# Key norm and group norm of the recurrent rounds in token form, spread back by products

## The reference, cut to what matters

```python
kk = heads(k * k_k)
kk = kk / jnp.maximum(jnp.sqrt(jnp.sum(kk * kk, axis=-1, keepdims=True)), 1e-12)
...
wkv = wkv7_scan(rh, heads(decay), kh, vh, -kk, kk * ah)
mean = jnp.mean(wkv, axis=-1, keepdims=True)
var = jnp.mean(jnp.square(wkv - mean), axis=-1, keepdims=True)
y = ((wkv - mean) * lax.rsqrt(var + GN_EPS)).reshape(B, S, RWKV_WIDTH) * ln_w + ln_b
bonus = jnp.sum(rh * kh * r_k, axis=-1, keepdims=True) * vh
return (y + bonus.reshape(B, S, RWKV_WIDTH)) * g
```

## Time and profile before

| what | value |
|---|---|
| median of 3 runs | 2893.79 us (2889.46 to 2896.81) |
| the profiled execution's own time | 2894.06 us |
| its span in the profile | 2892.3 us |
| TensorE (PE) busy | 2612.6 us, 90% |
| VectorE (DVE) busy | 1232.6 us, 43% |
| ScalarE (ACT) busy | 1094.6 us, 38% |
| GpSimd (POOL) busy | 811.4 us, 28% |

### The profile page before, as it was taken

How to read it: one execution, slowest core, us unless ns; L and a number is a source line. 1 busy time by engine, 2 the same in 40 slices (tenths; PEclk the granted TensorE clock), 3 DMA queues, 4 the chain that set the end, 5 groups by cost and what they waited for, 6 DMA issues and landing times. The chain is left out here.

```text
span 2892.3 us, 49485 instructions
## 1 busy us (share of the span) xinstructions
PE 2612.6 (90%) x19266; PEld 2052.9 (71%) x19266; DVE 1232.6 (43%) x1836; ACT 1094.6 (38%) x1686; POOL 811.4 (28%) x342
## 2 busy tenths in 40 slices
PE   8999979989898969669999999989978889898997
PEld 6887857868686857558878887768865567676665
DVE  3221024464646446442142221056836642674652
ACT  4433224333333323444434332243244432335441
POOL 3444423413232303004434444412210002232002
PEclk9999989999999989879999999999989999999999
DMA  4232322312121202013323223311110001122001
GB/s 135 88 100 90 101 71 86 90 51 86 55 90 51 88 25 80 8 47 102 102 73 95 94 94 102 101 37 51 58 44 1 1 8 51 45 73 65 1 1 65
DMA packets 51998, 188.39 MB, mean 65 GB/s; under 512 B 5760, under 2 KB 6016, under 8 KB 51712
## 3 DMA queue, kind: packets, MB, share of 16 engines
q1 hardware_dynamic: 50688, 181.74, 19.9%
q10 hardware_dynamic: 1152, 4.26, 0.4%
HBM read 183.88 MB, written 2.10 MB: 64 GB/s over the span
## 5 line engine op out<-in xcount | busy, mean ns | idle before, releaser
L2324 POOL TENSOR_TENSOR WLO<-RAW,WHI 128x1024 fp32r<-128x1024 f32 x334 | 806.3, 2414 | 2041.9 <-ACT WHI L297 2041.9
L297 ACT ACTIVATE WHI<-RAW 128x1024 fp32r<-128x1024 f32 x336 | 355.8, 1059 | 973.7 <-PE psum L311 774.4
L309 PE MATMUL psum<-HHI,WHI 128*128 128x512 f32 x1000 | 403.2, 403 | 41.7 <-DVE HLO L395 15.0
L310 PE MATMUL psum<-HLO,WHI 128*128 128x512 f32 x1000 | 396.5, 397 | 0.0
L311 PE MATMUL psum<-HHI,WLO 128*128 128x512 f32 x1000 | 396.4, 396 | 0.0
L309 PEld LDWEIGHTS psum<-HHI,WHI 128*128 128x128 f32 x1000 | 189.6, 190 | 91.6 <-issue 45.9
L309 PE MATMUL psum<-H2HI,WHI 128*128 128x512 f32 (+1 forms) x536 | 197.7, 369 | 31.2 <-DVE H2LO L393 21.6
L310 PEld LDWEIGHTS psum<-HLO,WHI 128*128 128x128 f32 x1000 | 189.4, 189 | 47.0 <-issue 3.2
L311 PEld LDWEIGHTS psum<-HHI,WLO 128*128 128x128 f32 x1000 | 189.2, 189 | 45.0
L310 PE MATMUL psum<-H2LO,WHI 128*128 128x512 f32 (+1 forms) x536 | 192.0, 358 | 0.0
L311 PE MATMUL psum<-H2HI,WLO 128*128 128x512 f32 (+1 forms) x536 | 191.7, 358 | 0.0
(11 more groups left out here) (381 smaller groups left out, 4995.9 us busy)
## 6 DMA issues: line engine op xcount, KB each, us to landing
RAW<-in_wstream SPq DMA_DIRECT2D x336, 512.0 KB, 3.5
X<-in_xT SPq DMA_DIRECT2D x8, 256.0 KB, 6.7
out_T<-OUT SPq DMA_DIRECT2D x4, 512.0 KB, 2.6
W3S<-in_lora ACTq DMA_DIRECT2D x5, 384.0 KB, 3.1
XC<-in_ctxT ACTq DMA_DIRECT2D x1, 1024.0 KB, 4.8
TRIG<-in_trig ACTq DMA_DIRECT2D x1, 960.0 KB, 6.8
FCC<-in_first SPq DMA_DIRECT2D x1, 576.0 KB, 8.6
LVL<-in_levels SPq DMA_DIRECT2D x1, 384.0 KB, 9.0
```

The lines of the kernel that those rows point to most:

```text
L297: act.activation(WHI[:, q % 2, :], RAW[:, q % 2, :], ACT.Copy).then_inc(rounded, 1)
L309: pe.matmul(out, tile_of(WHI, slot, u), hi(kt), start=first and last[0], stop=False)
L310: pe.matmul(out, tile_of(WHI, slot, u), lo(kt), start=False, stop=False)
L2324: pool.tensor_tensor(WLO[:, s, :], RAW[:, s, :], WHI[:, s, :].bitcast(F32), ALU.subtract)\
```

## The change

The two norms keep one number per token and head instead of a copy on each of 64 partitions. `token_sums` makes the tile of squares the stationary operand, 128 tokens at a time, and multiplies by two columns of the head mask: four products of 128 stationary columns and 2 moving ones, whose result is 128x8 (tokens on partitions; four blocks, two heads). Square root, maximum and reciprocal run on 128x8 in a new tile ROOT. `spread` brings the result back to 128x512 in PSUM by eight products, each with one column of ROOT repeated 64 times as stationary operand and the 128x128 identity as moving one. "kk" and "n0" then read their factor from PSUM.

```diff
+        ROOT = ra("ROOT", [P, 2, 2 * BLOCKS])
...
                 def low_ranks(p):
-                    pe.wait_ge(*A.before(f"sd_{p}", i))
-                    pe.wait_ge(*V.before(f"dd_{p}", i))
+                    pe.wait_ge(*V.before(f"n0_{p}", i))
...
+                def token_sums(name, p, src, *waits):
+                    for w in waits:
+                        pe.wait_ge(*w)
+                    for b in range(BLOCKS):
+                        mm = pe.matmul(SETS[p].B[0][:, 2 * b:2 * b + 2], src[:, b * P:(b + 1) * P], two_heads, start=True, stop=True)
+                    mm.then_inc(*S.inc(f"{name}_{p}"))
+                def spread(name, p, *waits):
+                    for w in waits:
+                        pe.wait_ge(*w)
+                    pe.sem_inc(tensor_ready)
+                    for b in range(BLOCKS):
+                        for h in range(2):
+                            mm = pe.matmul(SETS[p].B[0][h * HD:(h + 1) * HD, b * P:(b + 1) * P],
+                                           ROOT[:, p, 2 * b + h:2 * b + h + 1].to_broadcast([P, HD]), eye, start=True, stop=True)
+                    mm.then_inc(*S.inc(f"{name}_{p}"))
...
                 for p in TWO:
-                    head_sums("kkss", p, SETS[p].B[0], SETS[p].E1[:, :], A.at(f"kksq_{p}", i))
-                whole(streamed(1), streamed(2))
+                    token_sums("kkss", p, SETS[p].E1, A.at(f"kksq_{p}", i))
+                whole(streamed(1))
+                for p in TWO:
+                    spread("kkb", p, V.at(f"kkinv_{p}", i))
+                whole(streamed(2))
...
                 for p in TWO:
-                    head_sums("var", p, SETS[p].B[0], SETS[p].DSQ[:, :], A.at(f"dsq_{p}", i))
+                    token_sums("var", p, SETS[p].DSQ, A.at(f"dsq_{p}", i))
                 whole(tail)
+                for p in TWO:
+                    spread("varb", p, V.at(f"rinv_{p}", i))
...
-                    run("e3", p, d.E3[:, :], d.SG[:, :], ACT.Exp, V.at(f"cprev_{p}", i), V.at(f"kk_{p}", i), scale=-DECAY)
+                    run("e3", p, d.E3[:, :], d.SG[:, :], ACT.Exp, V.at(f"cprev_{p}", i), scale=-DECAY)
...
-                    run("kkn", p, d.E3[:, :], d.B[0], ACT.Sqrt, S.at(f"kkss_{p}", i))
+                    run("kkn", p, ROOT[:, p, :], d.B[0][:, 0:2 * BLOCKS], ACT.Sqrt, S.at(f"kkss_{p}", i))
...
-                    run("sd", p, SETS[p].E1[:, :], SETS[p].B[0], ACT.Sqrt, S.at(f"var_{p}", i), scale=1.0 / HD, bias=EPS[:, 1:2])
+                    run("sd", p, ROOT[:, p, :], SETS[p].B[0][:, 0:2 * BLOCKS], ACT.Sqrt, S.at(f"var_{p}", i), scale=1.0 / HD, bias=EPS[:, 1:2])
...
+                def unit_root(p):
+                    ts(f"kkmax_{p}", ROOT[:, p, :], ROOT[:, p, :], 1e-12, None, ALU.max, None, A.at(f"kkn_{p}", i))
+                    inverse(f"kkinv_{p}", ROOT[:, p, :], V.at(f"kkmax_{p}", i))
                 def unit_key(p):
-                    ts(f"kkmax_{p}", d.E3[:, :], d.E3[:, :], 1e-12, None, ALU.max, None, A.at(f"kkn_{p}", i))
-                    inverse(f"kkinv_{p}", d.E3[:, :], V.at(f"kkmax_{p}", i))
-                    stt(f"kk_{p}", d.KK[:, :], d.RKV[:, 1, :], col("k_k", i * 2 + p), d.E3[:, :], ALU.mult, ALU.mult, V.at(f"kkinv_{p}", i))
+                    stt(f"kk_{p}", d.KK[:, :], d.RKV[:, 1, :], col("k_k", i * 2 + p), d.B[0], ALU.mult, ALU.mult, S.at(f"kkb_{p}", i))
...
+                unit_root(0)
+                unit_root(1)
                 unit_key(0)
...
                 for p in TWO:
+                    inverse(f"rinv_{p}", ROOT[:, p, :], A.at(f"sd_{p}", i))
+                for p in TWO:
-                    inverse(f"rinv_{p}", d.E1[:, :], A.at(f"sd_{p}", i))
-                    tt(f"n0_{p}", dv, dv, d.E1[:, :], ALU.mult, V.at(f"rinv_{p}", i))
+                    tt(f"n0_{p}", dv, dv, d.B[0], ALU.mult, S.at(f"varb_{p}", i))
```

More of the change, by code:

```diff
@@ L601, in block_kernel @@
         ROWS = ra("ROWS", [4, ROW])
+        ROOT = ra("ROOT", [P, 2, 2 * BLOCKS])
         named = lambda p, *names: [f"{n}_{p}" for n in names]
-        rw_pe = named(0, "zw", "za", "g") + named(1, "zw", "za", "g") + ["kkss_0", "kkss_1", "bonus_0"]
+        rw_pe = named(0, "zw", "za", "g") + named(1, "zw", "za", "g") + ["kkss_0", "kkss_1", "kkb_0", "kkb_1", "bonus_0"]
         rw_pe += named(0, "toka", "tokb", "tokk", "tokv", "m1", "al", "m2") + ["bonus_1", "t1_0"] + named(1, "toka", "tokb", "tokk", "tokv", "m1")
@@ L609, in block_kernel @@
         rw_pe += [f"xt{LEVELS - 1}_1", "z_0", "turn4", "y_1", "q_0", "z_1", "gt_0", "q_1", "gt_1"]
-        rw_pe += [f"s{n}_{p}" for n in range(CHUNKS - 1) for p in TWO] + ["turn5", "o_0", "o_1", "mean_0", "mean_1", "var_0", "var_1"]
+        rw_pe += [f"s{n}_{p}" for n in range(CHUNKS - 1) for p in TWO] + ["turn5", "o_0", "o_1", "mean_0", "mean_1", "var_0", "var_1", "varb_0", "varb_1"]
         rw_act = named(0, "sg", "aa", "gg") + named(1, "sg", "aa", "gg") + ["kksq_0", "kksq_1", "pb0", "kkn_0", "kkn_1", "e1_0", "e2_0", "pb1"]
@@ L619, in block_kernel @@
             rw_dve += named(p, "dr", "r", "dv", "v", "csum", "cprev")
-        rw_dve += named(0, "kkmax", "kkinv", "kk", "kp", "rk", "rt", "bb", "at", "bt", "ktl", "bon")
+        rw_dve += named(0, "kkmax", "kkinv") + named(1, "kkmax", "kkinv")
+        rw_dve += named(0, "kk", "kp", "rk", "rt", "bb", "at", "bt", "ktl", "bon")
         first_level = ("al", "xi", "xi0", "m2a", "m2b", "xit", "xit0")
-        rw_dve += named(1, "kkmax", "kkinv", "kk", "kp", "rk") + ["m1a_0", "m1b_0"] + named(1, "rt", "bb", "at")
+        rw_dve += named(1, "kk", "kp", "rk") + ["m1a_0", "m1b_0"] + named(1, "rt", "bb", "at")
         rw_dve += named(0, *first_level) + named(1, "bt", "ktl", "bon", "m1a", "m1b") + ["x1_0", "xt1_0"]
@@ L627, in block_kernel @@
         rw_dve += [f"xt{LEVELS - 1}_1", "q_0", "gt_0", "q_1", "gt_1"] + [f"s{n}_{p}" for n in range(CHUNKS - 1) for p in TWO]
-        rw_dve += ["dd_0", "dd_1", "rinv_0", "n0_0", "n1_0", "n2_0", "yf_0", "rinv_1", "n0_1", "n1_1", "n2_1", "yf_1", "mod_sum", "mods"]
+        rw_dve += ["dd_0", "dd_1", "rinv_0", "rinv_1", "n0_0", "n1_0", "n2_0", "yf_0", "n0_1", "n1_1", "n2_1", "yf_1", "mod_sum", "mods"]
         def h_hi(t):
@@ L695, in rwkv_tensor @@
             e2 = lambda s: FCC[s, FC["eye2"]:FC["eye2"] + HD]
+            two_heads = heads.rearrange("p (h n) -> p h n", n=HD)[:, :, 0]
             unit = lambda t: lambda s, n: t[s, n * CHUNK:(n + 1) * CHUNK]
@@ L765, in tokens @@
                     pe.wait_ge(*V.at(f"ktl_{p}", i))
-                    pe.wait_ge(*A.at(f"kkn_{p}", i))
                     unit_products(unit(d.B[0]), unit(d.AR[:, 0, :]), lambda s, n: e2(s), f"toka_{p}")
```

## The result

The changed kernel takes 2863.13 us (median, 2860.44 to 2864.4) against 2892.99 for the kernel before: a ratio of 0.990, 95% interval 0.9886 to 0.9914. That is 30 us less; the forecast was 2892.0 and its range ended at 2879. The execution profiled took 2860.44 us, the fastest of its four, with a span of 2858.6.

What follows compares the result with a forecast made beforehand. TensorE fills most of a round; its idle lies largely at the seams, behind a relay of engines. Round 1 -0.6, three seams -0.5 each, last end +3.9: 1.8 us gained, 2892.0; own range 2888 to 2896, whole 2879 to 2897.

Steps and rivals of the forecast that it cites:

- makes POOL ask at 634.2: Start of a round: POOL's subtraction asks while VectorE is in cprev_1 until 634.5, with kkmax next.
- the meeting: Seams of rounds 2 to 4: kkmax comes while POOL subtracts and waits 2.4 us.
- The rule itself: VectorE beside POOL: a two-port operation, like one with two SBUF inputs, is held to POOL's end; kkmax taken as such.
- it is held: Seams: kkmax waits 2.4 us for POOL and each seam loses 0.5 us; chance 0.45.
- 0.3 of distance is thin: Seams: VectorE 0.3 us away from kkmax being through before POOL asks, which would give rival 2's time.
- rival 2: Seams: kkmax isn't held and the clock stays; 3.7 us gained per seam, 2879.4 us in all; chance 0.25.
- The end: End of round 4: mods and TensorE's start come 3.9 us earlier, at half clock as before.
- Round 1: Round 1: TensorE pays 0.3 us for sums and 1.9 for spreads, gets 1.6 back at m1_0; loses 0.6.
- n0, n1, spreads and the last wait: n0 escapes POOL (about 0.69 us), n1 is held (some 2.2); spread pairs take 1.9; MOD wait 10 or less.
- behind m1_0 nothing changes: Rest of each round after m1_0: no change, so a shift there is carried through the round.
- Rival 3: low_ranks behind the var spreads and streamed(2): TensorE loses its clock, 2 us a stretch; 2904 us; chance 0.06.

Runs made afterwards that it cites:

- early: The changed kernel with the var spreads moved ahead of the tail block's last two of eight units; 2866.67 us, ratio to before 0.9919.
- pad: The kernel before with 64 empty semaphore increments in TensorE's stream behind streamed(0) of each round; 2889.65 us, ratio to before 1.0007.
- after_b: The changed kernel run once more with the same code; 2866.87 us, ratio to before 0.9908.
- key_only: The changed kernel with its group norm put back, only the key norm in token form; 2882.79 us, ratio to before 0.998.
- filler: The kernel before with the 24 products of streamed block 0 done twice; 2894.16 us, ratio to before 1.0013.
- group_only: The changed kernel with its key norm and e3's wait for kk put back; 2875.0 us, ratio to before 0.9956.
- pad16: The kernel before with 16 empty semaphore increments in TensorE's stream behind streamed(0); 2894.57 us, ratio to before 1.0013.
- held: The changed kernel with one more reciprocal, 400 elements wide, on VectorE ahead of the first kkmax; 2876.56 us, ratio to before 0.9966.

## Why the prediction was wrong

**The step that failed at the seams** is "Rounding (0.3 behind it, 1.06 long) makes POOL ask at 634.2. VectorE, 3.9 earlier, is then in "cprev_1", until 634.5." VectorE's side was exact: from the end of yf to kkmax I had 15.7 us, measured 15.65 (611.56 to 627.21). TensorE's side was not: from yf's end to POOL's second ask 15.4 forecast, 18.1 measured (611.56 to 629.64). Of the 2.7 us, 2.2 lie in low_ranks: its idle at the loop's turn was 2.71 where I took 1.5 from a round in which long products covered it, and the two pairs took 7.1 us until the block (607.73 to 614.84) where I had 6.1, with the granted clock at 0.57 in 608 to 612. So POOL asked after kkmax instead of just before it, in all three seams (by 2.4, 0.6 and 2.5 us; the 0.6 is seam 2, where low_ranks ran at full clock). A small delay on TensorE's side saved a larger one on VectorE's. That was luck and no property of the change: early moves low_ranks forward by 1.3 us, and the meeting is there in two seams of three.

**The rule itself held.** The prediction took it from how a faster one-input operation reads; the Trainium skill (SBUF — State Buffer, the section on the two separate sides) calls the shared pair of ports an exclusive lock for a VectorE operation in a two-port mode. The runs agree that it is held to POOL's end, with 0.89 and 2.35 us for a maximum that takes 0.17 alone, and 1.95 for n1; that the maximum runs in such a mode no run shows directly. I had put 0.45 on "it is held", which bundled the rule with a meeting known to only 0.3 us. The sentence "0.3 of distance is thin" named it, but the error on TensorE's side alone was 2.7 us, so that I would now give the meeting no more than an even chance (an estimate).

**By its own steps.** With kkmax free the text's rival 2 gives 3.7 us per seam; measured against an undisturbed 51.0 they are 3.8, 4.3 and 3.7. (Seam 3 of before had 1.6 us of half clock in it, absent in pad.) The road wasn't quite rival 2's, which had the clock stay up: low_ranks lost it in two of the three seams. The end: 3.9 forecast, 4.3 measured. Round 1: key sums to m1_0 cost 0.45 us, 0.6 forecast. n0, n1, spreads and the last wait (7.44, "10 or less") came as written. Rival 2 as a whole, 2879.4, was still 16 us too high.

**The second step that failed** took the measured time out of the whole range: "behind m1_0 nothing changes, so a shift there is carried through the round". It put at nothing the steps' 10.9 us (8.5 in after_b). The profile of before showed it: 4.7 us of "issue" in front of one line, four times, and a clock of 0.50 behind the first (0.72 in 1026 to 1032 behind the last). I read those as a property of the state steps that the change doesn't touch. But 88 instructions ahead of them are a change to them, and key_only, pad and filler against group_only and pad16 show that a shift alone is worth 9 to 10 us of the steps. Rival 3 was right about one of its two places: low_ranks behind the var spreads lost its clock in seams 1 and 3 of after and in all three of after_b, for 1.65 us each where it had 2. In streamed(2) nothing was lost, and the sum had the wrong sign.

**Open:** why low_ranks is at half clock behind 2.5 to 3.1 us of idle in some seams and at full clock in others (held has 2.98, 2.85 and 2.63 at full clock, after_b 2.87, 2.79 and 2.93 at half); and why the stops in the steps differ between two executions of the same kernel.

## What to carry over

When two engines' paths decide a collision, add up the error of both sums before giving the meeting a chance; if it is larger than the distance, move the dependent work so that it has room (here the spreads, by 2.8 us, though no meeting has tested that room). Look for stalls that wait for nothing in dense stretches of short instructions: a change anywhere ahead of them in the same loop can make or remove them, so a gain of this kind has to be separated from the change's own by a shift without work. And take an optimisation's halves apart, then ask of each part of the time where it came from: the key part is worth 10.9 us beside the group part, and all of it is the shift of the stream, none the shorter norm.

## What I had not expected of the hardware

Empty semaphore increments on TensorE's queue are not free: 64 took 5.55 us in round 1. But that is no price for one, since 16 took no time that can be seen (in round 1 the key sums of pad16 start 13.13 us behind low_ranks, in before 13.08). A maximum over 8 elements per partition waits the whole 2.35 us for POOL, while a reciprocal beside it takes its 0.20 (early, 908.69, with POOL from 908.58 to 910.93). A faster engine can lose time by it: in filler the full clock at the key sums made POOL come 1.9 us sooner, counted from the var sums, and VectorE lost 2.0 us to it. The instruction loads stop TensorE in the state steps: one packet, and work again 2.2 to 2.8 us after it, where 48 more instructions ahead in the loop make the longest of these stops vanish and 16 don't. The loop's turn is of the same kind, with 1.7 to 2.2 us from the packet's end to the first product.
